# A ninth weight buffer, and state outputs stored by SyncE and ScalarE instead of GpSimd

## The reference

```
h = rmsnorm(x, norm_mix); proj = h @ w_in
o_hg, s_hg = hgrn2_mix(proj[..., :2048], state_hgrn)     # s_hg: an output, 8 x 4 x 128 x 128 for the samples
o_rw, s_rw = rwkv7_mix(proj[..., 2048:], state_rwkv)     # s_rw: an output, 8 x 8 x 64 x 64 for the samples
x = x + concat(o_hg, o_rw) @ w_out
hf = rmsnorm(x, norm_ffn)
top-4 of 32 experts per token, gates = softmax(top values)
for each expert e, on its tokens:
    gate, up = hf @ w_gate_up[e] + b_gate_up[e]          # 1024 x 2048
    y += gates[e] * (((clip(up) + 1) * clamped_glu(gate)) @ w_down[e] + b_down[e])   # 1024 x 1024
outputs: rmsnorm(x + y), s_hg, s_rw, and the last normalised rows, for prompt and samples
```

## Time and profile before

| | |
|---|---|
| time of three runs | 1248.23, 1248.78, 1252.48 us; median 1248.78 us |
| profiled execution | span 1244.8 us from its first to its last instruction; its time outside the span is not listed (the median of the runs is 4.0 us above this span) |
| PE busy | 1211.9 us, 97% |
| DVE, ACT, POOL busy | 460.2, 255.2, 39.6 us |
| DMA | 436.11 MB, 350 GB/s on average, 426 to 434 GB/s from about 340 us on |
| TensorE clock granted | 0.998 of full speed |

### The profile page before, as it was taken

One profiled execution on the slowest core, in us unless ns is written; L12 is line 12 of the kernel. 1 busy time (PEld: TensorE's weight loads), 2 busy tenths in 40 slices (PEclk: granted clock), 3 DMA queues, 4 the chain that ended last, 5 costly groups with the idle time before them and its releaser, 6 DMA issues.

```text
span 1244.8 us, 18279 instructions
## 1 busy us (share of the span) xinstructions
PE 1211.9 (97%) x7854; PEld 584.8 (47%) x7854; DVE 460.2 (37%) x958; ACT 255.2 (21%) x619; POOL 39.6 (3%) x94
## 2 busy tenths in 40 slices
PE   8999999999999999999999999999999999999997
PEld 5777776745443434444444434434443444343332
DVE  2356986754312331333233223313322233132224
ACT  2113432521311102111111111121111111111113
POOL 7000010000100000000000000000000000000000
PEclk9999999999999999999999999999999999999999
DMA  9732102484999999999999999999999999999994
GB/s 281 175 93 78 53 27 71 125 339 191 377 426 427 427 427 427 432 434 427 432 430 429 433 429 432 428 432 430 431 429 432 431 427 434 429 430 431 426 424 173
DMA packets 45244, 436.11 MB, mean 350 GB/s; under 512 B 9045, under 2 KB 24472, under 8 KB 29162
## 3 DMA queue, kind: packets, MB, share of 16 engines
q1 hardware_dynamic: 44036, 431.35, 83.8%
q0 software_dynamic: 1040, 3.54, 0.9%
q10 hardware_dynamic: 86, 0.02, 0.0%
HBM read 430.01 MB, written 4.89 MB: 349 GB/s over the span
## 4 chain that ended last, share of the span: by engine, by line
PE 77%; DMA 18%; DVE 3%; ACT 1%; issue 0%; SPq 0%; DVEq 0%; ACTq 0%
PE bank L1457 28%; PE bank L1491 14%; PE bank L812 10%; DMA ring<-in_w_gate_up 9%; PE bank L1432 7%; DMA mix<-in_w_gate_up 6%; PE bank L1521 4%; PE bank L1247 3%; DMA mix<-in_w_down 2%; PE bank L1482 2%; PE bank L1005 1%; PE bank L1512 1%; DVE mix L2316 1%; PE bank L839 1%; DMA hx<-in_state_shift 0%
## 5 line engine op out<-in xcount | busy, mean ns | idle before, releaser
L1457 PE MATMUL bank<-ring,mix 128*64 128x512 f32 x1568 | 355.5, 596 | 11.7 <-DMA ring<-in_w_gate_up 10.9
L1457 PEld LDWEIGHTS bank<-ring,mix 128*64 128x64 f32 x1568 | 108.7, 137 | 227.1 <-issue 216.6
L1491 PE MATMUL bank<-ring,mix 128*64 128x512 f32 x736 | 167.8, 598 | 0.0
L2674 DVE TENSOR_TENSOR hTb<-bank,w2a 128x512 f32<-128x512 f32 x32 | 22.1, 691 | 373.7 <-PE bank L1482 373.7
L812 PE MATMUL bank<-hTb,ring 128*128 128x320 f32 (+1 forms) x480 | 139.1, 443 | 1.3 <-issue 1.3
L1991 ACT ACTIVATE mix<-bank,nf 128x256 f32<-128x256 f32 x64 | 26.9, 471 | 458.9 <-PE bank L1432 458.9
L1457 PE MATMUL bank<-mix 128*64 128x512 f32 x480 | 112.1, 599 | 1.3 <-DMA mix<-in_w_gate_up 1.2
L812 PEld LDWEIGHTS bank<-hTb,ring 128*128 128x128 f32 x480 | 89.5, 191 | 39.6 <-issue 3.7
L2726 DVE TENSOR_TENSOR mix<-mix,bank 128x512 f32<-128x512 f32 x70 | 48.2, 689 | 161.3 <-PE bank L1521 161.3
L1491 PEld LDWEIGHTS bank<-ring,mix 128*64 128x64 f32 x736 | 49.7, 136 | 87.4 <-issue 83.3
L1432 PE MATMUL bank<-mix,hx 128*128 128x256 f32 x256 | 70.0, 416 | 0.0
(11 more groups left out here) (422 smaller groups left out, 1099.9 us busy)
## 6 DMA issues: line engine op xcount, KB each, us to landing
ring<-in_w_gate_up SPq DMA_DIRECT2D x34, 4096.0 KB, 27.1
ring<-in_w_down SPq DMA_DIRECT2D x17, 4096.0 KB, 28.8
ring<-in_w_gate_up SPq DMA_DIRECT2D x30, 2048.0 KB, 14.5
mix<-in_w_gate_up SPq DMA_DIRECT2D x12, 4096.0 KB, 25.8
mix<-in_w_down SPq DMA_DIRECT2D x6, 4096.0 KB, 29.0
ring<-in_w_down SPq DMA_DIRECT2D x11, 2048.0 KB, 16.5
ring<-in_w_in SPq DMA_DIRECT2D x15, 1024.0 KB, 6.2
mix<-in_w_gate_up SPq DMA_DIRECT2D x6, 2048.0 KB, 14.2
```

The lines of the kernel that those rows point to most:

```text
L1457: last_ = mm(b_[64 * half:64 * half + 64, :].rearrange("s (p q) -> s p q", q=4), toks, cols[:, half], start=(c == 0), stop=(c == KT - 1))
L1491: last_ = mm(b_[r:r + 64, :], lhs, w[:, o:o + NCOL], start=(j == 0 and q == 0), stop=(j == 1 and q == 3))
L2674: v.tensor_tensor(halves(gg), halves(banks[3][:, :]), bias(e, 0), ALU.add).then_inc(S("g1"), 1)
```

## The change

Two pieces only ever use the ninth buffer: 8 and 17 (`ONCE`). All other pieces go round the eight old buffers, which shifts them by one buffer from piece 9 on and by two from piece 18 on. `HELD[k]` is the piece that lay in the buffer before k. Piece 8 is issued right behind `brows`; piece 9 is now the one that is loaded in three parts (`FIRST`).

```diff
+ONCE = (8, 17)
+FIRST = 9
+def piece_slots():
+    slot, before, had, n = [], [], {}, 0
+    for k in range(len(PIECES)):
+        if k in ONCE:
+            s = NWS
+        else:
+            s = n % NWS
+            n += 1
+        slot.append(s)
+        before.append(had.get(s))
+        had[s] = k
+    return slot, before
+SLOT, HELD = piece_slots()
...
+        wslot.append(sb("spare_slot", [P, PIECE])[:, :])
...
+            sync.wait_ge(S("hs2_ready"), 1)
+            sync.dma_start(O[2][0, 0].rearrange("h k v -> k h v"), hs[:, :, :]).then_inc(S("hgrn_out"), 16)
             w_out = A["w_out"][0].rearrange("(c p) n -> p c n", p=P)
...
+            sync.wait_ge(S("hsend_ready"), 8)
+            sync.dma_start(O[5][0].rearrange("b h k v -> k b h v"), hs0).then_inc(S("hgrn_out"), 16)
             sync.wait_ge(S("hgrn_out"), 32)
...
-                if k > NWS:
-                    sync.wait_ge(S("w_used"), k - NWS + 1)
+                if HELD[k] is not None:
+                    sync.wait_ge(S("w_used"), HELD[k] + 1)
...
             load(brows, bg, "brow_in")
+            load_piece(ONCE[0])
+            sync.wait_ge(S("pst_ready"), 1)
+            sync.dma_start(O[3][0, 0].rearrange("h v k -> v h k"), pout[:, :].rearrange("p (h k) -> p h k", k=RN))\
+                .then_inc(S("prompt_state_out"), 16)
...
-            for q in range(4):
-                pool.wait_ge(S("sout_ready"), q + 1)
-                for c in range(2):
-                    pool.dma_start(ors[c][:, q], sout[q][64 * c:64 * c + 64].rearrange("p j (h k) -> p (j h) k", h=2))\
-                        .then_inc(S("rwkv_out"), 16)
...
+            def states_out():
+                ors = O[6][0].rearrange("(b c) h v k -> c v b h k", c=2)
+                act.wait_ge(S("sout_ready"), 4)
+                for q in range(4):
+                    for c in range(2):
+                        act.dma_start(ors[c][:, q], sout[q][64 * c:64 * c + 64].rearrange("p j (h k) -> p (j h) k", h=2))\
+                            .then_inc(S("rwkv_out"), 16)
...
                 sigmoid(e)
+                if e == 0:
+                    states_out()
...
-    nc = _bacc.Bacc("TRN2", target_bir_lowering=False, num_devices=1)
+    nc = _bacc.Bacc("TRN2", target_bir_lowering=False, num_devices=1, dynamic_dma_scratch_size=512)
```

More of the change, by code:

```diff
@@ L252 @@
 WIDE = range(PLACE["up", EW, 0], PLACE["up", NE - 1, 0])
+ONCE = (8, 17)
[13 more added lines that the diff above has]
+SLOT, HELD = piece_slots()
 def piece_counts():
-    out, n = [], [0] * NWS
+    out, n = [], [0] * (NWS + 1)
     for k in range(len(PIECES)):
-        s = k % NWS
+        s = SLOT[k]
         if k in WIDE and k % 2:
@@ L593, in load_piece @@
                     if k % 2 == 0:
-                        sync.wait_ge(S("w_used"), k + 1 - NWS + 1)
-                        load(wpair[k % NWS // 2], rows_in(kind, e, j, 2), f"w{k % NWS}_in")
+                        sync.wait_ge(S("w_used"), HELD[k + 1] + 1)
+                        load(wpair[SLOT[k] // 2], rows_in(kind, e, j, 2), f"w{SLOT[k]}_in")
                     return
-                if k == NWS:
+                slot_ = wslot[SLOT[k]]
+                if k == FIRST:
                     for x in range(2):
                         sync.wait_ge(S("unit_filled"), len(UNITS) + 1 + x)
-                        load(wslot[0][:, 1024 * x:1024 * x + 1024], rows_in(kind, e, j)[:, 1024 * x:1024 * x + 1024], ("w0_in", "mid_in")[x])
+                        load(slot_[:, 1024 * x:1024 * x + 1024], rows_in(kind, e, j)[:, 1024 * x:1024 * x + 1024], ("w0_in", "mid_in")[x])
                     sync.wait_ge(S("w_used"), 1)
-                    load(wslot[0][:, 2048:PIECE], rows_in(kind, e, j)[:, 2048:PIECE], "end_in")
+                    load(slot_[:, 2048:PIECE], rows_in(kind, e, j)[:, 2048:PIECE], "end_in")
                     return
-                if k > NWS:
-                    sync.wait_ge(S("w_used"), k - NWS + 1)
+                if HELD[k] is not None:
+                    sync.wait_ge(S("w_used"), HELD[k] + 1)
                 if k >= len(PIECES) - 2:
-                    load(wslot[k % NWS][:, 0:PIECE // 2], rows_in(kind, e, j)[:, 0:PIECE // 2], f"w{k % NWS}_in")
-                    load(wslot[k % NWS][:, PIECE // 2:PIECE], rows_in(kind, e, j)[:, PIECE // 2:PIECE], ("mid_in", "end_in")[j])
+                    load(slot_[:, 0:PIECE // 2], rows_in(kind, e, j)[:, 0:PIECE // 2], f"w{SLOT[k]}_in")
+                    load(slot_[:, PIECE // 2:PIECE], rows_in(kind, e, j)[:, PIECE // 2:PIECE], ("mid_in", "end_in")[j])
                 else:
-                    load(wslot[k % NWS], rows_in(kind, e, j), f"w{k % NWS}_in")
+                    load(slot_, rows_in(kind, e, j), f"w{SLOT[k]}_in")
             sync.wait_ge(S("unit_filled"), U("Y0", 2))
@@ L622, in _ @@
             load(bdr, A["b_down"][0], "bdr_in")
-            for k in range(NWS, len(PIECES)):
+            for k in range(FIRST, len(PIECES)):
                 if k == 60:
@@ L729, in _ @@
                 .then_inc(S("eye_ready"), 1)
-            pool.wait_ge(S("hs2_ready"), 1)
-            pool.dma_start(O[2][0, 0].rearrange("h k v -> k h v"), hs[:, :, :]).then_inc(S("hgrn_out"), 16)
             pool.wait_ge(S("unit_filled"), U("s0t", 4))
@@ L740, in _ @@
             ins.then_inc(S("qm_ready"), 1)
-            pool.wait_ge(S("hsend_ready"), 8)
-            pool.dma_start(O[5][0].rearrange("b h k v -> k b h v"), hs0).then_inc(S("hgrn_out"), 16)
-            pool.wait_ge(S("pst_ready"), 1)
-            pool.dma_start(O[3][0, 0].rearrange("h v k -> v h k"), pout[:, :].rearrange("p (h k) -> p h k", k=RN))\
-                .then_inc(S("prompt_state_out"), 16)
-            ors = O[6][0].rearrange("(b c) h v k -> c v b h k", c=2)
-            for q in range(4):
-                pool.wait_ge(S("sout_ready"), q + 1)
-                for c in range(2):
-                    pool.dma_start(ors[c][:, q], sout[q][64 * c:64 * c + 64].rearrange("p j (h k) -> p (j h) k", h=2))\
-                        .then_inc(S("rwkv_out"), 16)
             pool.wait_ge(S("shift_out"), 16 * (NS + 1))
@@ L1449, in arrived @@
                 pe.wait_ge(S(f"w{place}_in"), count)
-                return wslot[k % NWS]
+                return wslot[SLOT[k]]
             def up_chunk(b0, b1, toks, w, c, release=False):
@@ L1496, in down @@
                 w = arrived("down", e, j)
-                if e + j == 0:
+                if PLACE["down", e, j] == FIRST:
                     pe.wait_ge(S("mid_in"), 16)
@@ L1732, in last_down @@
                     pe.wait_ge(S(("mid_in", "end_in")[j_]), 32)
-                w_ = wslot[PLACE["down", last_e, j_] % NWS] if half_ else arrived("down", last_e, j_)
+                w_ = wslot[SLOT[PLACE["down", last_e, j_]]] if half_ else arrived("down", last_e, j_)
                 last_ = down_part(last_e % 2, j_, w_, last_e % 2, bGT, 2 * half_, 2 * half_ + 2)
```

## The result

The changed kernel takes 1264.64 us (median of 4 runs, 1263.99 to 1266.47), the kernel before, run beside it, 1249.33 us (4 runs, 1248.23 to 1252.48). The ratio is 1.0131, 95% interval 1.0114 to 1.0148. The two medians differ by 15.3 us; 1.0131 stands for 16.4. The profiled execution has a span of 1261.9 us, 17.1 us more than before, where 11 had been forecast.

What follows compares the result with a forecast made beforehand. PE sets the pace first, the weight stream the end, with 13.8 us of PE waits as slack. Stall 14 less 2.8 gives 11.2, say +11 on the 1244.8 us span: 1255.8; plus 4.0, say 1259.5 us; range 1246 to 1270.

Steps and rivals of the forecast that it cites:

- A: At expert 1's turn: ACT, held issuing its stores, stops PE for 14 us; 1255 to 1264 us, chance 0.42.
- A2: Rival: issuing doesn't hold ACT, which waits at `down_out(0)`; PE stops 26 us at expert 2's turn; 1272 us, chance 0.16.
- B: Rival: ACT's rows get several per turn, stores land within 20 us, no one waits; 1246 to 1249 us, chance 0.38.
- C: Rival: the ninth buffer's whole piece, 4.9 us, survives and the stores cost nothing; 1243.9 us, chance 0.04.
- The rate of ACT's rows: ACT's stores beside the weight stream: one 256 B row an engine per 0.634 us, 24 ns when alone.
- The room in the queue: ACT's DMA queue holds about 120 rows an engine, so four of the eight stores can be handed over at once.
- The price of the stall: PE, waiting for ACT's copies of expert 1, goes on at about 371 instead of 357.2 us: 14 us.
- The 2.8 us given back at piece 28: At piece 28 the queue gives up 2.8 us of PE's 14 us delay, so the stream ends 11.2 us later.
- The ninth buffer: Puts the stream 4.9 us ahead from piece 9; 2.8 us outlive piece 28, bounds 0 and 4.9.
- SP's three stores: Stores of hs and pout moved to SP: cost taken as 0; hs0 between -1.7 and +2 us.
- another dip: The ninth buffer's lower bound: a gain of 0 us instead of 2.8.

Runs made afterwards that it cites:

- e2: The kernel before with only the eight 128 KB state stores moved from POOL to ACT, eight buffers: 1263.39 us, ratio 1.0127.
- e1: The changed kernel with the eight state stores issued by SP behind piece 12 instead of by ACT: 1246.64 us, ratio 1.0000.
- e9: The changed kernel with three of the eight state stores on ACT and five in SP's queue behind piece 12: 1247.64 us, ratio 1.0003.
- e3: The changed kernel without the eight state stores and the waits for them (output unwritten): 1247.71 us, ratio 1.0003.
- e6: The kernel before without the eight state stores and the waits for them (output unwritten), eight buffers: 1247.95 us, ratio 1.0005.
- e5: The changed kernel without the eight state stores and their waits, ninth buffer used by pieces 8, 17, 26 and 35: 1246.28 us, ratio 0.9991.
- e10: e7 with the ninth buffer used by six pieces, up to piece 53, and 4 MB loads from expert 12 instead of 8: 1245.67 us, ratio 0.9989.
- e7: e5 with the eight state stores back, on SP, two ahead of each of pieces 12 to 15: 1245.89 us, ratio 0.9988.
- e8: The changed kernel with ACT's eight stores written as 512 rows of 2 KB instead of 4096 of 256 B: 1247.47 us, ratio 1.0000.
- e4: e1 with the ninth buffer used by four pieces (8, 17, 26, 35) instead of two: 1247.63 us, ratio 0.9999.

## Why the prediction was right, and where its sums were off

**The path: right.** The forecast's own case, A, came true: ACT held by its own issue, the copies of expert 1 late, PE stopped at L1500 (14.07 us, forecast 14), ACT free at 369.8 (369), the stream dry at about 367, the small packets gone within microseconds once it was dry. e2 and e1 show the eight stores on ACT as the only cause. A2 fell as a place (the wait was at expert 1's turn), B because the rows did not keep pace, C because the stores cost.

**The number: low, and helped a little by luck.** The span was to grow by 11 us and grew by 17.1. The time was forecast as 1259.5 us and measured as 1264.64, inside the whole range of 1246 to 1270, but just outside the 1255 to 1264 that A had for itself. The forecast added 4.0 us to the span, the distance of the median from one profiled execution. In every run on record the time is 2.0 to 2.2 us above its own span; the other 2 us are chance, between one execution and the median of three. Three terms were off: the clock, which was not in the sum (2.2 us), the gain of the buffer (2.8 foretold, nothing got), and about 1 us in small parts.

**The rate of ACT's rows: wrong in form.** I reckoned one row an engine in each 0.634 us from start to end. The rows show a burst of 77 an engine in 2 us, then one in 1.8 us, then one in 31 ns. The Trainium skill, page "DMA: Bandwidth & Descriptors", section "Queues, rings and completion order", has the engines go round their queues by whole packets of some 9 to 17 descriptors. This case's trace doesn't agree with any fixed turn: it has 125 packets of ACT's against 365 weight packets from 346 to 360 us, and 1232 against 36 in the burst. The forecast of 14 us came out nonetheless because the stall's end doesn't depend on this rate: ACT is freed by the stream's drying up, and that is set by SP's last issue at 357.64 and by what had been queued. e2 bears that out: there 195 packets of ACT's went from 346 to 360 us instead of 125, and the wait was still 14.0 us. A stall that comes out right with a wrong rate is luck as far as the rate goes. e9 was to test the rate and could not, since SP's small rows ran beside ACT's.

**The room in the queue: not shown.** I took 120 rows an engine. The fourth issue was held from 339.1 to 357.2, though by 344 us 6 + 1232 + 107 = 1345 packets had gone, 84 of the first 96 rows of an engine on average. An average over 16 engines hides how uneven they are: the third store landed only at 367.7, so at least one engine still had rows of it then. Which engine moved which packet isn't recorded. What fits is that an issue waits for the fullest of the 16, but no run here shows it.

**The price of the stall: too small by 2.2 us.** PE was 0.3 us late ahead of the stall (the row of L1509 ahead of it starts at 353.94 us, its like before at 353.63), waited 14.07, and went on 14.45 us late (371.66 against 357.21). When it reached L1475 at 378.47, it was 16.6 us late; in the kernel before these were the rows:

```profile
358.37 3.65 PE L1491 MATMUL bank<-ring,mix 128*64 128x512 f32 x16
361.86 1.89 PE L1457 MATMUL bank<-ring,mix 128*64 128x512 f32 x8
```

The 2.2 us in between are the clock, granted at 0.50 from 365 to 375 us and at 0.85 to 380. The prediction had no term for it. Two of the rows above carry most of it: 5.06 against 3.65 us, and 1.13 against 0.75. The Trainium skill, page "TensorE: Matmul & The Clock Gate", section "Part 1: The HAM clock gate", has idle time bring the slower clock; here the trace agrees, and I should have asked what 14 us of idleness do to it.

**The 2.8 us given back at piece 28: gone within two pieces.** The working was 14 - 2.8 = 11.2. By the landings the stream was 14.5 us late at piece 28 (443.2 against 428.7), 16.0 at piece 29 (449.9 against 434.0), 16.3 at piece 32 and 17.2 from piece 35 to the last. At 28, 16.6 - 2.8 = 13.8 was due, near enough. What failed is the next step, that the stream goes on at full rate from there. Landings of the changed kernel for the issues at 420.7, 427.9, 435.4 and 440.1 us, pieces 26 to 29:

```profile
L547 SPq DMA_DIRECT2D ring<-in_w_down x1: 328/328/328, 420.7 to 420.7; - x1
...
DMA to landing us min/median/max: 7.2/7.2/7.2
...
DMA to landing us min/median/max: 7.3/7.3/7.3
...
DMA to landing us min/median/max: 7.8/7.8/7.8
...
DMA to landing us min/median/max: 9.8/9.8/9.8
```

Three pieces in a row travel alone (7.2, 7.3, 7.8 us), and the engines are dry between them; the fourth starts into a queue that is filled unevenly and doesn't come 4.9 us after the third but 6.8. In e3, without any stall, it was 7.7. (That the queue is filled unevenly is my guess; the trace doesn't tell the engines apart.) Therefore the stream's lag became PE's lag, 16.3 against 16.6, and PE's waits for weights stayed at 13.5 us instead of falling by 3. The sum as it should have been: 0.3 + 14.1 + 2.2 + 0 = 16.6 us, against 17.1 measured between the two profiled executions; the two medians differ by 15.3.

**The ninth buffer: the size right at its bound, the value nothing.** The prediction gave it 2.8 us between 0 and 4.9. After the clipping at piece 28 2.6 us were left (e3); the 0 of the range, "another dip", is what the kernel got, and e3, e6 and e1 all lie within 0.1% of the kernel before. In e3 the buffer's last piece is used up by 397 us of 1245, and no lead is left behind piece 29. e5, with the buffer in use until about 487 us, carried 3.7 us past that place and lost most of them by 547; e10, in use until about 567, went past that place too, and in its profiled execution 4.1 of the 4.9 us arrived. By the times, e7 and e10 gain 0.1%, at the edge of what the runs can tell.

**SP's three stores: nothing, as forecast.** e1 and e3 carry them in just that place, and no wait of PE or ACT in either points to them.

## What to carry to other kernels

Before a store moves to the queue of an engine that computes, look at the number and length of its rows, not at its bytes: here 4096 rows of 256 B held ACT for 32.8 us and PE for 14.1, and 512 rows of 2 KB held ACT for 5.2 us and PE not at all. The same stores in the stream's own queue, issued by an engine that has time to wait, cost no time, whether in one go (e1) or in pairs (e7). A further buffer gives only as much lead as the shallowest point of the queue behind it lets through, so look at the shortest time from issue to landing after its last use. In e10's trace a lead lived on where the buffer stayed in use past that point, but its time is no better than e7's. And a stall long enough to lower PE's clock costs more than its length.

## What the runs showed of the hardware that was not expected

- A second hardware queue beside a full stream of 16 KB packets: 1232 packets of 256 B in 2 us (all 16 engines), then one an engine in 1.8 us, then one in 31 ns when the stream was dry. The burst was seen on ACT's queue in both kernels that issue all eight stores there (1232 packets from 341 to 343 us; 1154 in e2). Why it ends, and why the rate is one small to three large packets afterwards, stays open. Where both queues held rows of 256 B, they went one for one (1012 to 1018 in e9); rows of 2 KB went 274 to 333 weight packets (e8).
- The same 1.05 MB held up the stream by about 1.5 us from POOL (e6), by 5.4 to 8.3 us in SP's queue when issued in one go (e1 and e4 against e3 and e5), and by 1.3 us in four pairs (e7 against e5, at piece 17), each known to some 2 us. None of these costs is seen in the time.
- Issuing a DMA can take long: one of ACT's took 18.09 us, against 0.65 to 0.73 for the three ahead of it.
- After a piece that travels nearly alone the next one comes late: 7.7 us behind it in e3, 7.5 in e6, 7.2 in e5 and 6.8 in the changed kernel, where a running stream has 4.9. In e3 the DMA share was 1.00 from 424 to 434 us, but at 403 GB/s; the kernel before moved 426 in the same 10 us, at a share of 1.01. The cause is open.
